# Splitting the sample group's cached values: half of the low parts on GpSimd, and another order of work on three engines

## The reference

```python
def mem_attend(h, mem_k, mem_v, w_mq, w_mo):
    b_, T, _ = h.shape
    q = (h @ w_mq).reshape(b_, T, MEM_HEADS, MEM_HEAD_DIM)
    s = jnp.einsum('bthd,bmhd->bhtm', q, mem_k).astype(jnp.float32) * (MEM_HEAD_DIM ** -0.5)
    p = jax.nn.softmax(s, axis=-1).astype(mem_v.dtype)
    o = jnp.einsum('bhtm,bmhd->bthd', p, mem_v).reshape(b_, T, D_MODEL)
    return o @ w_mo
```

## Time and profile before

| | |
|---|---|
| median of three executions | 4281.14 us |
| the profiled execution | 4279.69 us, its span 4278.0 us |
| TensorE busy | 4077.9 us (95%) |
| VectorE busy | 2592.4 us (61%) |
| ScalarE busy | 1390.0 us (32%) |
| GpSimd busy | 714.2 us (17%) |
| the changed stage | from about 1162 to 1290 us of the span |

### The profile page before, as it was taken

One profiled execution on the slowest core, in us unless ns is written; L12 is line 12 of the kernel. 1 busy time (PEld: TensorE's weight loads), 2 busy tenths in 40 slices (PEclk: granted clock), 3 DMA queues, 4 the chain that ended last, 5 costly groups with the idle time before them and its releaser, 6 DMA issues.

```text
span 4278.0 us, 69824 instructions
## 1 busy us (share of the span) xinstructions
PE 4077.9 (95%) x26191; PEld 3935.2 (92%) x26191; DVE 2592.4 (61%) x4092; ACT 1390.0 (32%) x1876; POOL 714.2 (17%) x514
## 2 busy tenths in 40 slices
PE   8998979979889979999999999999999999999996
PEld 6788969979849979999999999999999999999996
DVE  3324232351453266666477556666679899898896
ACT  3433221132442132222355422222233333333333
POOL 0000020020000030044100001111123333344430
PEclk9989989989999999999999999999999999999998
DMA  6542222213542212233344599999999999999994
GB/s 224 196 117 55 82 59 79 78 50 118 197 138 79 78 54 77 97 117 121 113 171 169 195 315 355 354 350 355 355 339 403 397 411 409 394 400 396 402 384 135
DMA packets 495289, 943.10 MB, mean 220 GB/s; under 512 B 126372, under 2 KB 375904, under 8 KB 443032
## 3 DMA queue, kind: packets, MB, share of 16 engines
q1 hardware_dynamic: 443552, 567.36, 39.8%
q0 software_dynamic: 51616, 374.19, 21.8%
HBM read 866.63 MB, written 73.56 MB: 220 GB/s over the span
## 4 chain that ended last, share of the span: by engine, by line
PE 91%; DVE 4%; DMA 2%; ACT 2%; DVEq 1%; issue 1%; POOL 0%; SPq 0%; ACTq 0%
PE pl L1127 25%; PE pp L197 24%; PE pp L1186 12%; PE pt L1186 6%; PE pl L1186 6%; PE pp L1095 5%; PE pt L1104 2%; PE pp L792 2%; PE pt L792 1%; PE pl L792 1%; PE pp L859 1%; DMA kv<-in_cache_mem_k 1%; DMA raw<-in_w_mk 1%; PE pl L821 1%; PE pt L823 1%; PE pl L1046 1%
## 5 line engine op out<-in xcount | busy, mean ns | idle before, releaser
L1127 PE MATMUL pl<-h_hi,ut_hi 128*128 128x384 f32 x2048 | 734.7, 359 | 0.6 <-ACT ijt L1465 0.6
L1127 PE MATMUL pl<-h_hi,ut_lo 128*128 128x384 f32 x2048 | 692.1, 338 | 0.0
L1127 PE MATMUL pl<-h_lo,ut_hi 128*128 128x384 f32 x2048 | 691.3, 338 | 0.0
L1838 DVE TENSOR_TENSOR ut_lo<-pp,ut_hi 128x512 fp32r<-128x512 f32 x508 | 350.2, 690 | 483.3 <-ACT ut_hi L1418 479.1
L1418 ACT ACTIVATE ut_hi<-pp 128x512 fp32r<-128x512 f32 x508 | 304.1, 599 | 820.6 <-PE pp L1095 763.4
L212 DVE TENSOR_TENSOR w_lo<-raw,w_hi 128x2048 fp32r<-128x2048 f32 x120 | 274.8, 2291 | 424.0 <-ACT w_hi L207 424.0
L1490 ACT ACTIVATE v_hi<-v_raw 128x1024 fp32r<-128x1024 f32 x256 | 271.9, 1062 | 682.6 <-PE pl L1186 438.3
L1940 DVE TENSOR_TENSOR v_lo<-v_raw,v_hi 128x1024 fp32r<-128x1024 f32 x256 | 313.2, 1223 | 123.3 <-ACT v_hi L1490 122.6
L1127 PEld LDWEIGHTS pl<-h_lo,ut_hi 128*128 128x128 f32 x2048 | 387.1, 189 | 0.0
L1127 PEld LDWEIGHTS pl<-h_hi,ut_hi 128*128 128x128 f32 x2048 | 386.2, 189 | 0.8 <-ACT ijt L1465 0.8
L1127 PEld LDWEIGHTS pl<-h_hi,ut_lo 128*128 128x128 f32 x2048 | 384.7, 188 | 0.0
(11 more groups left out here) (387 smaller groups left out, 8257.7 us busy)
## 6 DMA issues: line engine op xcount, KB each, us to landing
u_raw<-in_peer_u SPq DMA_DIRECT2D x256, 512.0 KB
v_raw<-in_peer_v SPq DMA_DIRECT2D x256, 512.0 KB
p_f<-p_scr SPq DMA_DIRECT2D x256, 192.0 KB
raw<-in_w_in SPq DMA_DIRECT2D x24, 1024.0 KB, 5.6
g_scr<-gs POOLq DMA_DIRECT2D x6, 4096.0 KB, 13.6
raw<-in_w_mk SPq DMA_DIRECT2D x16, 1024.0 KB, 4.9
raw<-in_w_mv SPq DMA_DIRECT2D x16, 1024.0 KB, 4.8
raw<-in_w_out SPq DMA_DIRECT2D x16, 1024.0 KB, 5.9
```

Source lines behind the costliest of these rows:

```text
L1127: last = mm(pl[:, d, 0:N], w[:, d, k, :], x[:, k, S:S + N], start=(k == 0 and w is ut_hi and x is h_hi), stop=(k == KC - 1 and w is ut_lo))
L1838: tt(ut_lo[:, d, 4 * g:4 * g + 4, :], src.rearrange("p (c i) -> p c i", c=4), ut_hi[:, d, 4 * g:4 * g + 4, :].bitcast(F32), ALU.subtract). ...
```

## The change

On TensorE the prompt scores of part n and the turn of part n - 1 come first in round n, then the two sample units of the round together. Before, the scores stood between the two units and the turn behind them. ScalarE's and VectorE's lists follow this order: ScalarE does the exponentials, both `value_hi` copies of the next round and the copy to `ptt`; VectorE does the maximum, then the windows with the even half's `value_lo` between them, then the normalisation. The odd half's `value_lo` goes to GpSimd, as eight subtractions of 128x2048, each of which waits for both high halves of its sequence. The semaphore `vs_l` becomes one for each half. VectorE's split of the first `w_mo` panel moves from c = 10 to behind the loop over c.

```diff
-        vs_l = sem("vs_l")
+        vs_l = [sem("vs_l0"), sem("vs_l1")]
...
-                pe.wait_ge(vs_l, u + 1)
+                pe.wait_ge(vs_l[m], b + 1)
...
-            prompt_scores(0)
-            sample_turn()
-            for n in range(1, UNITS + 1):
-                sample_unit(2 * n - 2)
+            for n in range(UNITS + 1):
                 if n < UNITS:
                     prompt_scores(n)
-                sample_unit(2 * n - 1)
-                prompt_turn(n - 1)
+                if n == 1:
+                    sample_turn()
+                if n >= 1:
+                    prompt_turn(n - 1)
+                for u in SAMPLE_UNITS.get(n, ()):
+                    sample_unit(u)
...
-            value_hi(0)
-            sample_probs()
-            prompt_exp(0)
-            value_hi(1)
-            for n in range(1, UNITS + 1):
+            for n in range(UNITS + 1):
+                if n == 1:
+                    sample_probs()
                 if n < UNITS:
-                    value_hi(2 * n)
-                    prompt_exp(n)
-                prompt_probs(n - 1)
-                if n < UNITS:
-                    value_hi(2 * n + 1)
+                    act.wait_ge(ps_max, n + 1)
...
+                for u in SAMPLE_UNITS.get(n + 1, ()):
+                    value_hi(u)
+                if n >= 1:
+                    k = n - 1
+                    act.wait_ge(ps_tr, k + 1)
...
-            sample_norm()
-            prompt_max(0)
-            value_lo(0)
-            dve.wait_ge(ss_pt, 1)
-            prob_window(0)
-            prob_window(1)
-            prompt_norm(0)
-            value_lo(1)
-            for n in range(1, UNITS + 1):
+            for n in range(UNITS + 1):
                 if n < UNITS:
-                    prob_window(2 * n)
-                    value_lo(2 * n)
-                    prompt_max(n)
-                    prob_window(2 * n + 1)
-                    prompt_norm(n)
-                    value_lo(2 * n + 1)
+                    dve.wait_ge(ps_done, n + 1)
...
+                if n == 0:
+                    sample_norm()
+                for u in SAMPLE_UNITS.get(n, ()):
+                    if n == 1 and u == 0:
+                        dve.wait_ge(ss_pt, 1)
+                    prob_window(u)
+                    if u % MT == 0:
+                        value_lo(u)
+                if n < UNITS:
+                    dve.wait_ge(ps_exp, 2 * (n + 1))
...
-                if c == 10:
-                    dve_split(dve, num(MO0))
...
+            dve_split(dve, num(MO0))
             residual_norm(MO0, norm2, KC)
...
+            for b in range(DB):
+                pool.wait_ge(vs_h, MT * b + 2)
+                g.tensor_tensor(vs_lo[:, b % 2, 1, :], kv[:, b % 2, 1, :], vs_hi[:, 1, :].bitcast(F32), ALU.subtract)\
+                    .then_inc(vs_l[1], 1)
             pool_less_mean(pool, norm2)
```

More of the change, by code:

```diff
@@ L1351, in value_hi @@
                 f(vs_hi[:, m, :], kv[:, b % 2, m, :], ACT.Copy).then_inc(vs_h, 1)
[L1353 to L1364, removed]
-            value_hi(0)
-            sample_probs()
-            prompt_exp(0)
-            value_hi(1)
-            for n in range(1, UNITS + 1):
-                if n < UNITS:
-                    value_hi(2 * n)
-                    prompt_exp(n)
-                prompt_probs(n - 1)
-                if n < UNITS:
-                    value_hi(2 * n + 1)
+            for n in range(UNITS + 1):
+                if n == 1:
+                    sample_probs()
+                if n < UNITS:
+                    act.wait_ge(ps_max, n + 1)
+                    if n >= 2:
+                        act.wait_ge(ps_tr, n - 1)
+                    for x in range(2):
+                        f(pr[n % 2][:, x, :], score_bank(n)[:, x, :], ACT.Exp, bias=pst[:, n % 2, 1, x:x + 1], scale=ASCALE,
+                          accum_out=pst[:, n % 2, 2, x:x + 1]).then_inc(ps_exp, 1)
+                for u in SAMPLE_UNITS.get(n + 1, ()):
[3 more added lines that the diff above has]
+                    act.wait_ge(ps_tr, k + 1)
+                    f(ptt[k // 2][:, :, k % 2 * 2 * P:(k % 2 + 1) * 2 * P], pt[k % 2][:, :].rearrange("p (m t) -> p m t", m=MT),
+                      ACT.Copy).then_inc(ps_pt, 1)
             act.wait_ge(sv_done, DB * MT)
@@ L1752, in _ @@
-            prob_window(1)
-            prompt_norm(0)
-            value_lo(1)
-            for n in range(1, UNITS + 1):
-                if n < UNITS:
-                    prob_window(2 * n)
-                    value_lo(2 * n)
-                    prompt_max(n)
-                    prob_window(2 * n + 1)
-                    prompt_norm(n)
-                    value_lo(2 * n + 1)
+                tt(vs_lo[:, b % 2, m, :], kv[:, b % 2, m, :], vs_hi[:, m, :].bitcast(F32), ALU.subtract).then_inc(vs_l[m], 1)
@@ new lines, in _ @@
+            for n in range(UNITS + 1):
+                if n < UNITS:
+                    dve.wait_ge(ps_done, n + 1)
+                    st_n = pst[:, n % 2]
+                    if n >= 2:
+                        dve.wait_ge(ps_exp, 2 * (n - 1))
+                    nc.vector.tensor_reduce(st_n[:, 0, :], score_bank(n), AX.X, ALU.max)
+                    dve.drain()
+                    ts(st_n[:, 1, :], st_n[:, 0, :], -ASCALE, None, ALU.mult).then_inc(ps_max, 1)
+                if n == 0:
[8 more added lines that the diff above has]
+                    dve.wait_ge(ps_exp, 2 * (n + 1))
+                    nc.vector.reciprocal(st_n[:, 3, :], st_n[:, 2, :])
+                    dve.drain()
+                    tt(pr[n % 2][:, :, :], pr[n % 2][:, :, :],
+                       st_n[:, 3, :].rearrange("p (x m) -> p x m", m=1).to_broadcast([P, 2, MEM]), ALU.mult).then_inc(ps_p, 1)
```

## The result

The changed kernel takes 4323.74 us (median of 4 executions, 4319.63 to 4331.74) where the kernel before took 4283.02 beside it (median of 4): a ratio of 1.0096, 95% interval 1.0080 to 1.0112, or 34 to 48 us longer. The forecast was 4312, 31 us longer, in a range of 4295 to 4326. Run once more on another chip it was 4324.85 against 4292.18, ratio 1.0081 (1.0067 to 1.0095), 33 us longer. Before it is 1161.94 to 1290.20, 128.3 us. After it is 1160.13 to 1324.02, 163.9 us, 35.6 longer. The profiled executions are 4279.69 and 4318.80 us.

A forecast was written before the change was run, and what follows sets the result against it. TensorE's operand supply bounds the kernel; rounds grow from 10.5 to 14.55 us. Units +29.0, `v_two` -1.2, panel split +1.9 and its clock +1.65 make 31.3 us on 4281.14: 4312, range 4295 to 4326.

The forecast's parts named there:

- the path: Sample-unit rounds: odd copy, GpSimd's odd subtraction, VectorE's window and even subtraction, then 16 matmuls; 14.55 us with lowered clock, against 10.5.
- the likeliest case: Whole kernel: GpSimd and VectorE take turns and idle TensorE loses clock; 4312 us, own range 4302 to 4323, chance 62%.
- the clock: TensorE after idling: each gap of 2.8 us or more lowers the granted clock and costs 1.65 us.
- GpSimd's price: Odd half's 128x2048 subtraction on GpSimd: 4.5 us, bounded by 3.8 and 5.0; VectorE does it in 2.29.
- VectorE held up: VectorE's window subtraction or cast is stretched to GpSimd's end by an exclusive lock, so the even subtraction waits behind it.
- Rival (a): Sample-unit rounds: GpSimd and VectorE do not hold each other up; rounds 12.65 us with clock, total 4297; 10%.
- a round without it: A middle round from odd unit to odd unit, before any loss of clock: 12.9 us.
- Rival (b): Sample-unit rounds: the lock holds but TensorE's clock stays up; rounds 12.9 us, total 4299; 12%.
- (d): Lower clock lasts longer, all 16 value matmuls at half speed; rounds 16.4 us, total 4324 or more; 8%.
- The first round: First scores to unit 1's end: 5.8 us later, including 1.65 for the clock after a gap of 6 us.
- Behind the units: After unit 15: earlier `v_two` -1.2 us, uncovered split of the first `w_mo` panel +1.9, its clock loss +1.65.
- rival (c): Not slower: engines do not block and TensorE keeps its clock; rounds 11.0 us, total 4283; 8%, 3 for a gain.

The follow-up runs named there:

- the two moves: Kernel with the even subtraction first, plus ScalarE's even copy ahead of the exponentials and the odd window ahead of the maximum: 1.0013 of the kernel before.
- the run that fills the gap: Changed kernel plus five unread fp32 products on TensorE behind the turn in rounds 2 to 7: 1.0059 of the kernel before.
- the order alone: Changed kernel's new queue order, but odd low halves subtracted on VectorE behind the odd window, none on GpSimd: 1.0026 of the kernel before.
- the version without GpSimd at the end: New order, even low half ahead of the maximum, odd one on VectorE behind it, panel split back at c = 10: 0.9974 of the kernel before.

## Why the prediction was right, point by point

The time came out in the forecast's range, and the path that it named is the one in the trace. It came out near the upper end: the median of 4323.74 is 2 us under 4326, and just above the 4302 to 4323 that I gave the likeliest case. What the sum had too small is the clock.

**The path.** TensorE waits for the even low part in every middle round, and GpSimd's operation begins 2 us after the odd unit: both as forecast (rounds of 14.55 us on average in the first profile). The loads' waits are gone and gave nothing back.

**GpSimd's price** was forecast at 4.5 us, from 544- and 1280-column rows; it is 4.50 to 4.53 in all eight. The bounds of 3.8 and 5.0 weren't needed.

**VectorE held up.** The forecast put the wait on the window's subtraction or its cast. It fell on the operation before them, the scaling of the maximum, which has one operand. The even subtraction starts at GpSimd's end all the same, so the sum didn't change. The exponentials start late too (ScalarE waits 4.15 us for the maximum in these rounds), which has slack. Rival (a), no holding up, is excluded by the stretched rows. My reading of the earlier trace rows as turns was looser than I wrote: the two engines' operations there were 1.12 and 0.49 us longer, and the other's take 1.33 and 0.73. The later runs show it better: with GpSimd in the old order a two-operand operation of 0.69 us took 5.03, up to half a microsecond behind GpSimd's end; and with the even half first, and then with the two moves, a GpSimd subtraction begun 0.44 us before VectorE's ended took 4.85 us instead of 4.50, one begun 1.63 us before took 6.05.

**The clock** is the term that was mis-sized. I priced a gap at 1.65 us from gaps of up to 4.5 us. Behind gaps of 5.4 us it costs 1.7 and 2.9 in turn, 2.1 on average by the run that fills the gap. Over six rounds that is 2.7 us more than forecast; 1.8 more come from a round without it, 13.2 instead of 12.9, and 0.6 from the last, 10.0 instead of 9.4. Together they are the 5.1 us by which the seven rounds (101.85 against 96.7) were longer. Rival (b), a clock that stays up, is excluded; (d), a clock down through all 16 matmuls and rounds of 16.4, is not far off in the longer rounds of 15.8. My rule, that each gap of 2.8 us or more costs 1.65, held for this stage of the kernel before but is no rule: with GpSimd in the old order gaps of 2.89 and 3.28 us cost nothing, with the order alone 3.22 us cost 1.7 or 2.9, and with the even subtraction first one of 1.84 us cost 1.7. What decides it the runs don't show.

**The first round** was forecast 5.8 us longer from the first scores to the end of unit 1, and is 4.9 (22.85 against 17.99). That is partly luck: the scores ran at the clock of 1.00 there and at 0.66 in the kernel before. Like with like, in the repeated execution, it is 6.9 (24.9). The 1.1 us more than forecast fit the clock again: behind the gap of 6.16 us it has 0.57 over 7 us, which is 3.0 us where I took 1.65.

**Behind the units.** `v_two` gave back 1.1 us (forecast 1.2). From the values to the panel it is 3.55 us more (37.79 against 34.24), forecast 1.9. The split's own part is 1.9, measured by moving it back; the remaining 1.7 is in the values themselves: from 1294 to 1298 the clock is 0.57, which costs 1.7, and 1.00 on both sides (0.95 over 1287 to 1322). I had not counted a drop there. It has no gap just ahead: TensorE ran the first 8 matmuls of the values and 32 small ones of 64x32 (L1035) at 1.00 before it. The kernel before ran the same sequence at 1.00, and so did the one with the even subtraction first; the second execution of the changed kernel and the version without GpSimd at the end had the drop. What sets it off stays open. The panel's slow start was forecast at 1.65 and is 1.7.

**The sum.** Stage 35.6 and panel 1.7 make 37.3, against 31.3 forecast; of the 6.0 us, 2.7 are the clock in the rounds and 1.7 in the prompt values, 2.4 the rounds without it, 0.1 the rest, less 0.9 in the first round. Like with like it is 38.1 and 1.7, 39.8, 8.5 over the forecast. The medians gave 41 on one chip and 33 on another; the kernel before was not profiled on the second, so where 7 us went there stays open. In the first pair of profiles 39.1 us lie between the spans; 36.2 of them are there at the expert layer's first matmuls, and the last 3 come behind 3200 us. Of these 1.8 are a stretch at the lower clock (0.91 over 3230 to 3250, where the kernel before keeps 1.00); for the rest I have no cause to name.

**Not slower, rival (c),** needed VectorE to be free of GpSimd. The chain of scores, maximum, window, subtraction and units that I gave as its floor, 11.0 us and 12.65 with the clock, is close to what the run without GpSimd took: 12.0 to 13.7.

## What to carry to other kernels

In hand-ordered queues a cheap-looking swap moves an instruction behind a wait that it has nothing to do with; write down, for each engine, what the first urgent instruction behind a wait is, and place that one ahead (here one such move took 36 us off the stage, 31 off the total). Work sent to GpSimd is not free for VectorE: even a two-number operation (0.17 us alone) lasted until GpSimd's ended, so let VectorE issue its urgent work first. An idle stretch of TensorE can be paid twice, once as waiting and once at the lower clock: in the stage's middle rounds here every gap of 4.5 to 5.4 us cost another 1.5 to 2.9 us, gaps of 1.8 to 3.6 us sometimes as much and sometimes nothing. So put a range on that price, and compare traces only where the same stretches ran at the same clock.

## What the runs showed of the hardware that I had not expected

- A TENSOR_SCALAR of two columns with one operand in SBUF took 2.35 us beside a GpSimd subtraction and 1.49 beside a GpSimd memset, instead of 0.17; a CAST of 16 columns took 4.30. A TENSOR_TENSOR with two operands in SBUF wasn't slowed by a memset (2.28 us), but another, 128x512, took 5.03 us instead of 0.69 beside a GpSimd subtraction. A TENSOR_REDUCE from PSUM kept its 0.69 us beside one.
- A second such operation stood in the queue at the same time: beside the memset both TENSOR_SCALAR (1203.90) and the CAST behind it show as busy until 1205.4.
- Behind equal gaps of 5.41 us the lower clock (1.2 of 2.4 GHz) lasted for 8 and for 13 of the 16 value matmuls in turn, and with 1.1 us of gap, TensorE kept busy, for none. Behind equal gaps of 3.3 us (GpSimd in the old order) it came once and once not, and the same first scores, behind the same short gaps, ran at 0.66 in ten of the twelve profiled executions and at 1.00 in two.
